# Turning the gated blocks of a two-layer decoder trunk: TensorE transposes exchanged for 32x32 transposes on VectorE and small transfers

## What is computed

```python
def swiglu(x, w_in, w_out):
    g, u = jnp.split(x @ w_in, 2, axis=-1)
    return (jax.nn.silu(g) * u) @ w_out

# reference, layer 0 (S5), then layer 1 (attention over one block of 256)
h = h + 0.5 * swiglu(rmsnorm(h, ffn1_norm), ffn1_w_in, ffn1_w_out)
h = h + s5_mixer(rmsnorm(h, mix_norm), ...)          # diagonal state space model, then a gated linear unit
h = h + 0.5 * swiglu(rmsnorm(h, ffn2_norm), ffn2_w_in, ffn2_w_out)
k, v = split(rmsnorm(h, kv_norm) @ w_kv)             # before layer 1's first FFN
h = h + 0.5 * swiglu(...); h = h + attention(rmsnorm(h) @ w_q, k, v) @ w_o; h = h + 0.5 * swiglu(...)
out = rmsnorm(h, final_norm)
```

## Time and profile before

| | |
|---|---|
| median of 3 runs | 973.5 us (972.28 to 973.59) |
| the profiled execution's own time | 969.86 us |
| its span in the trace | 967.7 us |
| PE, PEld, DVE, ACT, POOL busy | 955.9, 790.2, 597.8, 499.8, 189.5 us |
| DMA: moved, mean, share of 16 engines | 169.35 MB, 175 GB/s, 54.5% (queue 1) |
| TensorE clock granted | 0.998 of full speed |

### The profile page before, as it was taken

The page is one execution under the profiler, slowest core; times in us unless marked ns, Lnnn a source line. Parts: engine busy times, 40 slices in busy tenths (PEclk is TensorE's granted clock), DMA queues, the critical chain, the costliest instruction groups (busy, mean ns, idle before and its releaser), DMA issues.

```text
span 967.7 us, 15102 instructions
## 1 busy us (share of the span) xinstructions
PE 955.9 (99%) x6110; PEld 790.2 (82%) x6110; DVE 597.8 (62%) x744; ACT 499.8 (52%) x711; POOL 189.5 (20%) x235
## 2 busy tenths in 40 slices
PE   9999999999999999999999999999999999999997
PEld 7888888788788888888888888888888888888886
DVE  5565779889765554656555555555557555656544
ACT  7554544576555454545544454554458454545441
POOL 4899999800000000000000000000060000000000
PEclk9999999999999999999999999999999999999999
DMA  9766555520455655565566666656651366555551
GB/s 347 269 184 197 181 174 174 175 69 5 142 187 193 194 178 194 184 208 183 166 198 196 193 177 196 191 177 195 188 182 45 111 198 193 186 187 192 179 169 43
DMA packets 47557, 169.35 MB, mean 175 GB/s; under 512 B 5505, under 2 KB 5505, under 8 KB 47489
## 3 DMA queue, kind: packets, MB, share of 16 engines
q1 hardware_dynamic: 47056, 167.79, 54.5%
q10 hardware_dynamic: 432, 0.61, 0.2%
HBM read 167.33 MB, written 1.05 MB: 174 GB/s over the span
## 4 chain that ended last, share of the span: by engine, by line
PE 88%; DVE 8%; issue 2%; ACT 1%; DMA 1%; SPq 0%; POOLq 0%; POOL 0%; DVEq 0%; ACTq 0%
PE ps L1252 85%; DVE w_lo L931 2%; PE ps L1257 2%; DVE scan L1158 1%; DVE tmp L1087 1%; PE ps L1284 1%; DMA raw<-in_in 1%; DVE rot_b L1165 1%; DVE rot_a L1145 1%; DVE rot_b L1147 1%; ACT w_hi L652 0%; DVE rot_in L1154 0%; DVE states L1172 0%; PE ps L1297 0%; ACT pr L881 0%
## 5 line engine op out<-in xcount | busy, mean ns | idle before, releaser
L931 DVE TENSOR_TENSOR w_lo<-raw,w_hi 128x1024 fp32r<-128x1024 f32 x311 | 399.7, 1289 | 307.0 <-ACT w_hi L652 305.7
L652 ACT ACTIVATE w_hi<-raw 128x1024 fp32r<-128x1024 f32 x311 | 328.4, 1059 | 305.9 <-PE ps L1252 303.2
L1252 PE MATMUL ps<-w_hi,x_hi 128*128 128x512 f32 x896 | 352.4, 393 | 0.9 <-DVE w_lo L931 0.6
L1252 PE MATMUL ps<-w_hi,x_lo 128*128 128x512 f32 x896 | 349.3, 390 | 0.0
L1252 PE MATMUL ps<-w_lo,x_hi 128*128 128x512 f32 x896 | 349.2, 390 | 0.0
L1252 PEld LDWEIGHTS ps<-w_hi,x_hi 128*128 128x128 f32 x896 | 168.4, 188 | 37.2 <-DVE w_lo L931 1.4
L1252 PEld LDWEIGHTS ps<-w_hi,x_lo 128*128 128x128 f32 x896 | 168.3, 188 | 35.2
L1252 PEld LDWEIGHTS ps<-w_lo,x_hi 128*128 128x128 f32 x896 | 168.5, 188 | 34.0
L1252 PE MATMUL ps<-w_hi,hid_hi 128*128 128x512 f32 x352 | 138.1, 392 | 1.0 <-DVE w_lo L931 1.0
L1252 PE MATMUL ps<-w_lo,hid_hi 128*128 128x512 f32 x352 | 137.2, 390 | 0.0
L1252 PE MATMUL ps<-w_hi,hid_lo 128*128 128x512 f32 x352 | 137.2, 390 | 0.0
(11 more groups left out here) (151 smaller groups left out, 599.6 us busy)
## 6 DMA issues: line engine op xcount, KB each, us to landing
raw<-in_in SPq DMA_DIRECT2D x175, 512.0 KB, 4.3
raw<-in_out SPq DMA_DIRECT2D x88, 512.0 KB, 3.4
raw<-in_glu SPq DMA_DIRECT2D x16, 512.0 KB, 4.3
raw<-in_k SPq DMA_DIRECT2D x8, 512.0 KB, 4.4
raw<-in_v SPq DMA_DIRECT2D x8, 512.0 KB, 4.1
raw<-in_q SPq DMA_DIRECT2D x8, 512.0 KB, 4.4
raw<-in_o SPq DMA_DIRECT2D x8, 512.0 KB, 4.0
xt<-in_xt SPq DMA_DIRECT2D x4, 256.0 KB, 5.6
```

The costliest lines, as they stand in the source:

```text
L652: act.activation(w_hi[:, gu % WS, :], raw[:, gu % RAW, :], ACT.Copy)\
L931: dve.tensor_tensor(w_lo[:, gu % WS, :], raw[:, gu % RAW, :], w_hi[:, gu % WS, :].bitcast(F32), ALU.subtract)\
L1252: return pe.matmul(o, w, x, start=start, stop=stop, skip_group_check=True)
```

## The change

The gated blocks are turned in pairs and without PE. VectorE transposes a block in place (`dve.transpose`), which turns each square of 32x32 but leaves the squares where they are. SP then moves the squares to their places with transfers from SBUF to SBUF into `hid_lo`: 16 for a pair, each 32 partitions by 8 rows of 32 elements (128 bytes), four behind each of four weight loads. ScalarE copies `hid_lo` to `hid_hi` and VectorE subtracts in place. The same is done with all of k (it lands in `k_sb`) and with the first parts of h in glu and in phases 4 and 8 (they land in `x_lo`), by way of one tile `sheet`, which takes the place of `kq`. Phase 10's h, the later parts of the others and q stay on PE.

```diff
+MOVE_BEHIND = 8
+SHEETS = [(2, 0), (2, 1), (4, 0), (5, 0), (5, 1), (8, 0)]
+BY_ROWS = [(2, 2), (2, 3), (4, 2), (4, 3), (8, 2), (8, 3), (10, 0), (10, 1), (10, 2), (10, 3)]
+MOVED = 16 * QS * QS
...
 def high_behind(p, phases, b, j):
-    if p.name == "in" and b in BATCHES[1:] and j >= 2:
-        first = b - BATCH + 2 * (j - 2)
-        return [(p, first), (p, first + 1)]
...
+    if p.name == "in" and b >= 3 and b % 2 and j in (1, 2):
+        return [(p, b - 4 + j)]
+    if p.name == "out" and b == 0 and j in (1, 2, 6):
...
+            def move_hidden(p, b, q):
+                k, n = pair_number(p, b), pair_end(p, b) + 1 - b
+                sp.wait_ge(hid_squares, p.hid0 + b + n)
+                for c in range(QS):
+                    sp.dma_start(places(b, n, q, c), pieces(p, b, n, q, c)).then_inc(hid_moved[k % 2], 16)
...
+            moves = {p.unit0 + (pair_end(p, b) + 1) * p.upb + MOVE_BEHIND + q: (p, b, q)
+                     for p in phases if p.name == "in" for b in range(0, p.blocks, 2) for q in range(QS)}
...
             for gu in range(10, len(units)):
                 load(gu)
+                if gu in moves:
+                    move_hidden(*moves[gu])
+                if gu in sheet_moves:
+                    move_sheet(*sheet_moves[gu])
...
             def high_hidden(p, b):
-                act.wait_ge(hid_turned, p.hid0 + min(b // BATCH * BATCH + BATCH, p.blocks))
-                act.activation(halves(hid_hi[:, 2 * b:2 * b + 2, :].rearrange("p f x -> p (f x)")),
-                               turned_block(b), ACT.Copy).then_inc(hid_hi_done, 1)
+                k = pair_number(p, b)
+                act.wait_ge(hid_moved[k % 2], MOVED * (k // 2 + 1))
+                act.activation(hid_hi[:, 2 * b:2 * b + 2, :], hid_lo[:, 2 * b:2 * b + 2, :].bitcast(F32),
+                               ACT.Copy).then_inc(hid_hi_done, 1)
...
             def drain_kq(p, b, toks=range(TT)):
...
+                    if p.name == "k":
+                        act.wait_ge(sheet_moved, MOVED * SHEETS.index((p.n, b)))
...
             def gated(p, b):
...
+                if p.name == "in":
+                    dve.wait_ge(drained, p.drained0 + TT * (b + 1))
+                    whole = prod_of(p, b).rearrange("p t x -> p (t x)")
+                    dve.transpose(whole, whole).then_inc(hid_squares, 1)
             def low_hidden(p, b):
...
+                dve.wait_ge(hid_hi_done, p.hid0 + b + 1)
+                part = hid_lo[:, 2 * b:2 * b + 2, :]
+                dve.tensor_tensor(part, part.bitcast(F32), hid_hi[:, 2 * b:2 * b + 2, :].bitcast(F32),
+                                  ALU.subtract).then_inc(hid_ready, 1)
...
+            def turned_sheet(p, b):
+                dve.wait_ge(kq_drained, p.kq0 + TT * (b + 1))
+                whole = sheet[:, :, :, :].rearrange("p i t x -> p (i t x)")
+                dve.transpose(whole, whole).then_inc(sheet_squares, 1)
...
-                        if j == 1:
-                            turn_hidden(*batch_behind(p, phases, b))
```

More of the change, by code:

```diff
@@ L108, in follow_ups, with pair_end, pair_number, high_behind @@
     return [(phases[p.n - 1], phases[p.n - 1].blocks - 1, j)] if chained else []
[L111 to L115, removed]
-        f = phases[p.n - 1]
-        return f, range(BATCHES[-1], f.blocks)
-    return p, range(0)
-def high_behind(p, phases, b, j):
-    if p.name == "in" and b in BATCHES[1:] and j >= 2:
-        first = b - BATCH + 2 * (j - 2)
-        return [(p, first), (p, first + 1)]
[L126 to L129, removed]
+def pair_end(p, b):
+    return min(b // 2 * 2 + 1, p.blocks - 1)
+def pair_number(p, b):
+    return p.hid0 // p.blocks * ((p.blocks + 1) // 2) + b // 2
+def high_behind(p, phases, b, j):
+    if p.name == "in" and b >= 3 and b % 2 and j in (1, 2):
+        return [(p, b - 4 + j)]
+    if p.name == "out" and b == 0 and j in (1, 2, 6):
+        f = phases[p.n - 1]
+        return [(f, f.blocks - 4 + j if j < 3 else f.blocks - 1)]
     return []
 def low_behind(p, phases, b, j):
[L135 to L140, removed]
+    if p.name == "in" and b >= 3 and b % 2 and j in (2, 3):
+        return [(p, b - 5 + j)]
+    if p.name == "out" and b == 0 and j in (2, 3, 7):
+        f = phases[p.n - 1]
+        return [(f, f.blocks - 5 + j if j < 4 else f.blocks - 1)]
     return []
@@ L258, in w_columns, with sheet_tile, sheet_pieces, sheet_places @@
             return w2[:, :, :, PPT * d:PPT * d + PPT, :].rearrange("p r s g j -> p (r s) g j")
-        def prod_of(b):
-            i = b % BATCH
-            return prod[:, i] if i < 2 else prod2[:, i - 2]
+        def sheet_tile(q):
+            return sheet[:, :, q, :]
+        def sheet_pieces(tiles, q, c):
+            return sheet[Q * q:Q * q + Q, 0:tiles].rearrange("p i t (c x) -> p c (i t) x", x=Q)[:, c]
+        def sheet_places(n, b, tiles, q, c):
+            to = k_sb if n == 5 else x_lo[X_OF[n][-1][1]]
+            return to[Q * c:Q * c + Q, tiles * b:tiles * b + tiles, :].bitcast(F32)\
+                .rearrange("p i (t q x) -> p q (i t) x", t=TT, x=Q)[:, q]
+        def turned_x(n, c, i):
+            if (n, c) in BY_ROWS:
+                return ps[:, TA + turned[n, c] % 2, i * TOK:i * TOK + TOK]
+            return x_lo[X_OF[n][-1][1]][:, 2 * c + i, :].bitcast(F32)
+        def sheet_of(n, c):
+            return SHEETS.index((n, c if n == 2 else c // 2))
+        def high_unit(n, c):
+            if (n, c) in BY_ROWS:
+                return 1
+            return 5 if n == 2 else 5 + c
+        def turned_now(p, b, j):
+            if p.name == "glu":
+                return [c for c, at in ((b - 1, j + p.upb), (b, j)) if c >= 0 and at == high_unit(p.n, c)]
+            if p.n in (4, 8, 10):
+                return [c for c in (2 * b, 2 * b + 1) if j == high_unit(p.n, c)]
+            return []
+        def pair_of(k):
+            return prod if k % 2 == 0 else prod2
+        def prod_of(p, b):
+            return pair_of(pair_number(p, b))[:, b % 2]
+        def tile_of(p, b, q):
+            return prod_of(p, b).rearrange("p i (t x) -> p t i x", x=P)[:, q]
+        def pieces(p, b, n, q, c):
+            return pair_of(pair_number(p, b))[Q * q:Q * q + Q, 0:n]\
+                .rearrange("p b t (a c x) -> p c (b t a) x", a=2, x=Q)[:, c]
+        def places(b, n, q, c):
+            return hid_lo[Q * c:Q * c + Q, 2 * b:2 * (b + n), :].bitcast(F32)\
+                .rearrange("p i (t q x) -> p q (i t) x", t=TT, x=Q)[:, q]
         def halves(a):
             return a.rearrange("p (b h x) -> p b h x", h=2, x=HP)
-        def turned_block(b):
-            at, col = KT + b % BATCH // 2 * 2, b % 2 * HB
-            return ps[:, at:at + 2, col:col + HB].rearrange("p h (b x) -> p b h x", x=HP)
         def z_place(d):
@@ L303, in trunk @@
         act_ready = sem("act_ready")
-        hid_turned = sem("hid_turned")
+        hid_squares = sem("hid_squares")
+        hid_moved = [sem(f"hid_moved{i}") for i in range(2)]
         hid_hi_done = sem("hid_hi_done")
@@ L391, in trunk @@
             sq_at[n] = total, parts
-        turned = {nc_: i for i, nc_ in enumerate((n, c) for n in (2, 4, 8, 10) for c in range(DT // 2))}
+        turned = {at: t for t, at in enumerate(BY_ROWS)}
         NORM = {0: 1, 3: 2, 5: 3, 6: 3, 7: 3, 9: 4, 11: 5}
```

134 lines of the change are left out of this document (66 added, 68 removed).

## The result

The changed kernel takes 977.23 us (median of 5 runs, 976.81 to 978.39), the kernel before, on the same chip, 972.28 us (5 runs, 970.35 to 973.59). The ratio is 1.0055, 95% interval 1.0044 to 1.0066: **slower by 0.55%**, where 960.6 was forecast. The profiled execution has a span of 976.4 us, against 967.7. The profiles differ by 8.7 us and the medians by 5.0 only: the profiled execution of the kernel before was one of its fastest (969.86 us), that of the changed kernel its slowest (978.39).

What follows compares the result with a forecast made beforehand. TensorE was taken to set the pace outside the S5 part. Span: 967.7 - 16.0 (transposes) + 2.1 (S5 start) + 1.0 (k) = 954.8 us; that gain of 12.9 makes the median 960.6, range 953.5 to 980.

Steps and rivals of the forecast that it cites:

- The new wait: ScalarE's hid_hi waits up to 4 us for a pair's sixteenth transfer; 2.9 us margin before TensorE needs weights, no stall.
- Leaves TensorE, 16.0 behind S5: Transposes removed from TensorE: 19.8 us in sum, 3.8 in phase 0 ahead of S5 and 16.0 behind it.
- The S5 start, +2.1: Before S5, VectorE's two-SBUF-operand hid_lo slows GpSimd by 3.0 us (0 to 6.6); unit 18's w_lo ends 2.1 us behind TensorE.
- k, +1.0: At k, one sheet serves two blocks, so the second drains late and TensorE waits; charged 1.0 us (0 to 4).
- Glu "inside the margin": Glu's second sheet waits like k's, but with transfers half as long, so inside the margin; no stall charged.
- Rival (a): Moved pieces arrive late (issue above 0.78 us or landing over 6), stalling TensorE once per pair; 999 us at 0.9; chance 0.25.

Runs made afterwards that it cites:

- Experiment 1: Changed kernel with hid_hi and hid_lo of every gated pair one unit (2.7 us) later in ScalarE's and VectorE's order; 967.21 us, ratio 0.9956 to the kernel before.
- experiment 8: Changed kernel with later pair reads and phase 0's gated blocks, glu's and phase 4's h and k back on TensorE; 960.36 us, ratio 0.9864 to the kernel before.
- experiment 7: Changed kernel with later pair reads and phase 0's gated blocks and glu's and phase 4's h back on TensorE, k still moved; 960.76 us, ratio 0.9883.

## Why the prediction was wrong

**The step that failed is "The new wait", in its last clause: "a margin of 2.9 us, and no stall".** The sum behind it was made once, for an undisturbed pair. The first pairs of phases 3, 7 and 11 bear it out (no stall, the moves landing 16.0 to 17.2 us behind the unit's start against 16.0), with two errors that nearly cancel: issues and loads 1.4 to 2.1 us longer, the landing 0.8 to 1.3 shorter. For the third pair of phase 0 the traces show three terms in its place. The squares were taken as ready 2.1 us behind the unit's start, although a wait of ScalarE pushes VectorE's work behind it, the next transpose among it: 3.1 us. Issues and loads took 13.5 us, not 10.9: 2.6, of which the earlier landing gave 0.9 back. And w_lo was taken at 1.23 us, although its row up to 2.31 stood beside it and was used for the S5 term only: 1.1. Together they turned +2.9 into about -3, and TensorE stood still. Backlog alone takes the margin away in phase 7, where GpSimd runs nothing. Experiment 1 gives one unit of margin back and 1.0% of the time with it.

Term by term, against a forecast of -12.9 us of span and +8.7 between the two profiles (+5.0 between the medians):

- **Leaves TensorE, 16.0 behind S5.** Right. Phases 3 to 12, freed of stalls in experiment 8, are 12.6 us shorter than before: 2.77 in each of phases 3, 7 and 11, where two batches of 32 were priced at 2.72; 1.14 in phases 4 and 12, where the 24 was priced at 1.11; and 2.03 in phase 8, where h's 0.90 comes on top.
- **The S5 start, +2.1.** It was 13.9. Its mechanism was right and small: alone it costs 3.0 us of time and 4.5 on GpSimd's chain between two profiles, where 3.0 was taken. But in the changed kernel GpSimd isn't late at all: its last cp ends at 176.1 us, 2.6 earlier than before. A likely reason, not shown, is that VectorE had fallen behind and so got in its way less: by 176 us it had begun 46 w_lo since 30 us, not 50, and 4 of its table steps, not 9. S5 waited for TensorE. The 11.8 us missing here are the stalls of phases 0 and 1 and the slow clock behind them.
- **k, +1.0.** 1.5 in the changed kernel (k and v 0.3 us shorter, for 1.8 of transposes), and 4.2 in experiment 7 (2.4 us longer), the slow clock included. Its range of 0 to 4 nearly held both.
- **Glu "inside the margin", phase 4's sheet at nothing.** Wrong: I took a glu transfer of 128 pieces as half as long. Its issue takes 585 ns at the least, like one of 256. Glu, phase 3 and phase 4 are 6.1 us longer together than without a stall (2.4, 2.0 and 1.7), and phases 7 and 8 another 2.1 by late pairs.
- The rest lies within the S5 layer, 1.5 us longer in this profile. It isn't explained; the layer varies by 2.5 us over the ten traces.

Rival (a) named the right place, ScalarE's wait holding back a weight copy, but only part of the trigger: no pair's sixteen issues took over 0.67 us on the mean, and no landing over 4.9, though single issues reached 1.75. Its price per pair was right in kind; its 0.25 was too little, as it asked only whether a transfer is slow and not whether the start of the count slips. It put most of its chance at over 2% slower, and 0.55% came.

## What to carry to other kernels

A margin counted for one undisturbed pair has to be counted again for the pairs behind it, with the backlog that the wait itself leaves, and where another engine stretches the instructions in it, with those rows' maxima. A wait that sits in an in-order queue in front of feeding work is worth moving back until its margin is a whole unit; here that was worth 1% for a table of a few numbers. And where an engine is shared, apply a change stage by stage: the same edit gave 2.8 us in one phase and cost 8.2 in another.
